# Query projection of cross attention: heads 1 to 3 by seven products of halves per pair of tiles

## The reference, cut to what matters

```python
def cross_attention(xn, mk, mv, w_xq, xq_norm, w_xo):
    bsz, t, _ = xn.shape
    q = rmsnorm((xn @ w_xq).reshape(bsz, t, N_HEADS_X, HEAD_DIM_X), xq_norm)
    s = jnp.einsum('bqhd,bkhd->bhqk', q, mk).astype(jnp.float32) * (HEAD_DIM_X ** -0.5)
    p = jax.nn.softmax(s, axis=-1).astype(mv.dtype)
    o = jnp.einsum('bhqk,bkhd->bqhd', p, mv).reshape(bsz, t, N_HEADS_X * HEAD_DIM_X)
    return o @ w_xo
```

## Time and profile before

| | |
|---|---|
| Median of three runs | 1535.73 us |
| Span of the profiled execution | 1531.5 us |
| Its own time | the span and what lies around it; the median is 4.2 us above the span |
| TensorE matmul busy | 1507.3 us, 98% |
| VectorE busy | 970.2 us, 63% |
| ScalarE busy | 592.3 us, 39% |
| GpSimd busy | 243.6 us, 16% |
| DMA | 189.33 MB, 124 GB/s |
| Granted TensorE clock | 9 tenths or more in all 40 slices |

### The profile page before, as it was taken

How to read it: one execution, slowest core, us unless ns; L and a number is a source line. 1 busy time by engine, 2 the same in 40 slices (tenths; PEclk the granted TensorE clock), 3 DMA queues, 4 the chain that set the end, 5 groups by cost and what they waited for, 6 DMA issues and landing times.

```text
span 1531.5 us, 26752 instructions
## 1 busy us (share of the span) xinstructions
PE 1507.3 (98%) x10928; PEld 1447.3 (95%) x10928; DVE 970.2 (63%) x1370; ACT 592.3 (39%) x1021; POOL 243.6 (16%) x322
## 2 busy tenths in 40 slices
PE   8999999999999999998999999999999999999998
PEld 8999999997778999986899999999999999999998
DVE  7736777757777443457443896666665597547653
ACT  7521031146775221235322743333334344334332
POOL 1010000002100100000000054455444310010110
PEclk9999999999999999999999999999999999999999
DMA  8425111103102533022212244443344865354562
GB/s 279 142 98 176 54 42 42 45 1 103 68 29 71 163 127 136 15 73 71 85 73 85 85 158 158 150 151 128 133 177 177 325 230 181 117 178 121 185 213 100
DMA packets 64063, 189.33 MB, mean 124 GB/s; under 512 B 7888, under 2 KB 12040, under 8 KB 63808
## 3 DMA queue, kind: packets, MB, share of 16 engines
q1 hardware_dynamic: 39392, 95.30, 19.0%
q0 software_dynamic: 24560, 92.45, 16.8%
HBM read 138.58 MB, written 54.12 MB: 126 GB/s over the span
## 4 chain that ended last, share of the span: by engine, by line
PE 50%; DMA 4%; DVE 2%; issue 1%; ACT 1%; SPq 0%; DVEq 0%
PE ps L2836 20%; PE ps L2857 19%; PE ps L424 8%; DMA a<-wdn 3%; PE ps L2709 1%; PE ps L2676 1%; DVE B_lo L1985 0%; DMA r_raw_a<-quads_d 0%; DVE neg_max L1946 0%; PE ps L2687 0%; PE ps L2716 0%; DVE xpt_lo L1992 0%; ACT x_scores L1288 0%; ACT B_hi L1329 0%; DVE w_lo_b L411 0%
## 5 line engine op out<-in xcount | busy, mean ns | idle before, releaser
L424 PE MATMUL ps<-A_hi,w_hi 128*128 128x364 f32 (+1 forms) x768 | 171.2, 331 | 0.3 <-DVE Y L1554 0.3
L424 PE MATMUL ps<-A_lo,w_hi 128*128 128x364 f32 (+1 forms) x768 | 169.0, 328 | 0.0
L424 PE MATMUL ps<-A_hi,w_lo 128*128 128x364 f32 (+1 forms) x768 | 168.3, 327 | 0.0
L387 ACT ACTIVATE w_hi<-w_raw 128x1024 fp32r<-128x1024 f32 x42 | 44.2, 1058 | 286.2 <-PE ps L424 185.7
L424 PEld LDWEIGHTS ps<-A_hi,w_hi 128*128 128x128 f32 x768 | 130.8, 188 | 7.3 <-issue 6.6
L424 PEld LDWEIGHTS ps<-A_lo,w_hi 128*128 128x128 f32 x768 | 132.8, 188 | 0.0
L424 PEld LDWEIGHTS ps<-A_hi,w_lo 128*128 128x128 f32 x768 | 132.6, 188 | 0.0
L391 DVE TENSOR_TENSOR w_lo<-w_raw,w_hi 128x1024 fp32r<-128x1024 f32 x42 | 51.1, 1221 | 101.9 <-ACT w_hi L387 101.9
L2836 PE MATMUL ps<-t_hi,wq_hi 128*128 128x272 f32 x480 | 99.3, 288 | 0.3 <-issue 0.3
L2836 PE MATMUL ps<-t_lo,wq_hi 128*128 128x272 f32 x480 | 99.2, 288 | 0.0
L2836 PE MATMUL ps<-t_hi,wq_lo 128*128 128x272 f32 x480 | 99.1, 288 | 0.0
(11 more groups left out here) (327 smaller groups left out, 3570.4 us busy)
## 6 DMA issues: line engine op xcount, KB each, us to landing
w_raw<-slabs SPq DMA_DIRECT2D x67, 512.0 KB, 4.0
quads_d<-quad_sum POOLq DMA_DIRECT2D x64, 272.0 KB, 2.9
w_raw<-wdn POOLq DMA_DIRECT2D x32, 512.0 KB, 4.1
r_raw_a<-quads_d SPq DMA_DIRECT2D x56, 272.0 KB, 3.1
r_raw_b<-quads_d SPq DMA_DIRECT2D x56, 272.0 KB, 3.2
quads_d<-hid_stage POOLq DMA_DIRECT2D x48, 272.0 KB, 2.8
Y<-xT POOLq DMA_DIRECT2D x16, 546.0 KB, 4.8
y_d<-Y POOLq DMA_DIRECT2D x16, 546.0 KB, 3.2
```

The lines of the kernel that those rows point to most:

```text
L387: e.activation(WH[:, par], RAW[:, par], ACT.Copy).then_inc(s.w_hi, 1)
L424: ins = e.matmul(PS[:, 3 * par + c, 0:n_], wt[:, wpar, w], xt[:, col:col + n_], start=(first and n == 0 and m == 0), stop=(last and n == l ...
```

## The change: what it does

Tiles 0 and 1 (head 0) stay plain tiles. Tiles 2 to 7 (heads 1 to 3) become three pairs of seven products each, 21 products, with the functions of the MLP's first product or copies of them. The sums of the activations are made with `norm_x` before the first pair, in the same memory that the MLP uses later. The weight sums and copies of products lie in parts of `A` that the products don't read (`XSW`, `XTMP`). All pairs share one weight buffer `RAW`: the first half of the next pair is loaded after four weight sums and four low parts of this pair, the second half after all seven low parts. The products run in plain order 0 to 6. The squares of heads 0 to 2 go into tiles 6 and 7 of `Y`. VectorE makes all the low parts, of the sums, of the weights and of the activations. The stat and the broadcasts of head h now stand between products, in banks 0 or 6 (`stat_bank`). The keys and values of memory (`load_kv`) of heads 0 to 2 are loaded when 17, 19 and 21 products are done, where they were loaded ahead of tile 2 before. Tile counts after the projection are six lower (`C_XO`, `C_UP`), and counts of the MLP's products start after those of the projection (`X_PROD` and the like).

```diff
+N_XPAIR = 3
+N_XPROD = 7 * N_XPAIR
 # SyncE
+            for p in range(N_XPAIR):
+                for half in range(2):
+                    if p == 0:
+                        sp.wait_ge(s.w_lo, S_XQ + half + 1)
+                    elif half == 0:
+                        sp.wait_ge(s.sp_sum, 4 * p)
+                        sp.wait_ge(s.sp_lo, 7 * p - 3)
+                    else:
+                        sp.wait_ge(s.sp_lo, 7 * p)
+                    sp.dma_start(RAW[:, half], slabs[S_XQ + 2 + 2 * p + half]).then_inc(w_in[half], 16)
             for h in range(3):
+                sp.wait_ge(s.prod, 17 + 2 * h)
                 load_kv(h)
...
 # ScalarE
+            quad_scaled(1, "norm_x", S_OUT + 8)
+            t_hi(0, 0)
             act_root(e, cnt, D)
+            quad_scaled(3, "norm_x", S_OUT + 8)
+            xleft_hi(0)
+            t_hi(1, 0)
             act_bcast(e, cnt, RSTD)
+            t_hi(2, 0)
+            xleft_hi(1)
+            xleft_hi(2)
+            xprod_copy(0)
+            xsquares(0)
+            xleft_hi(3)
+            xprod_copy(1)
+            t_hi(3, 0)
+            xleft_hi(4)
+            xprod_copy(2)
+            xleft_hi(5)
+            act_root(e, cnt, 256, bank=stat_bank(0))
+            cnt.bc += 2
+            xleft_hi(6)
+            for n in range(7, N_XPROD):
+                p, i = divmod(n, 7)
+                xprod_copy(n - 4)
+                xleft_hi(n)
+                if i == 3:
+                    xsquares(p)
+                if i == 5:
+                    act_root(e, cnt, 256, bank=stat_bank(p))
+                    cnt.bc += 2
...
-            for i in range(8):
-                if i < 6:
-                    act_split(e, S_XQ + i + 2, i % 2, S_XQ + i + 1)
...
 # VectorE
+            t_raw(0, "norm_x", 0, 0)
+            t_raw(1, "norm_x", 0, 0)
+            t_lo(0, 0)
             dve_recip(e, cnt)
             cnt.bc += 2
+            t_raw(3, "norm_x", 0, 0)
+            xleft_lo(0)
+            t_raw(2, "norm_x", 0, 0)
             e.wait_ge(s.bc_used, cnt.used(cnt.bc))
-            for i in range(8):
-                if i < 6:
-                    dve_split(e, S_XQ + i + 2, i % 2)
...
+            xevac(0)
+            xevac(1)
+            xleft_sum(1)
+            xleft_sum(2)
+            xleft_lo(1)
+            t_lo(1, 0)
+            xleft_lo(2)
+            xleft_sum(4)
+            xleft_lo(3)
+            xleft_lo(4)
+            t_lo(2, 0)
+            xleft_sum(5)
+            xleft_lo(5)
+            xcombine(3)
+            dve_recip(e, cnt)
+            t_lo(3, 0)
+            xleft_lo(6)
+            xcombine(4)
+            xq_nrm(0, 0)
+            xleft_lo(7)
+            xcombine(5)
+            xq_nrm(0, 1)
+            for n in (3, 4, 5):
+                xscale(n)
+            for n in (8, 9):
+                xleft_sum(n)
+                xleft_lo(n)
+            for n in range(10, N_XPROD):
+                p, i = divmod(n, 7)
+                xcombine(n - 4)
+                if n + 1 < N_XPROD:
+                    xleft_sum(n + 1)
+                xleft_lo(n)
+                xscale(n - 4)
+                if i == 5:
                     dve_recip(e, cnt)
+                if p == 2 and i < 2:
+                    xq_nrm(1, i)
...
 # TensorE, after tiles 0 and 1
-            for h in range(3):
-                xq_tile(2 * h + 2)
-                xq_stat(h)
...
+            for n in range(N_XPROD - 1):
+                p, i = divmod(n, 7)
+                xproduct(n)
+                if i == (2 if p == 0 else 1):
+                    if p == 1:
+                        e.wait_ge(s.u_rel, 4)
+                    xq_stat(p)
+                    n_rc += 1
+                if i == (4 if p == 0 else 3):
+                    pe_bcast(e, cnt, 0, rc_wait(n_rc), lo=stat_bank(p))
+                if i == (5 if p == 0 else 4):
+                    pe_bcast(e, cnt, 1, lo=stat_bank(p))
...
+            xscores(0)
+            xproduct(N_XPROD - 1, (0,))
+            xscores(1)
+            xproduct(N_XPROD - 1, (1,))
+            xscores(2)
+            xproduct(N_XPROD - 1, (2, 3))
```

More of the change, by code:

```diff
@@ L1273, in _, with quad_scaled @@
             for par in range(2):
-                residual(S_OUT, 0, par, "norm_x", 8)
+                residual(S_OUT, S_OUT, 0, par, "norm_x", 8)
             with e.Fori(1, 4) as i:
                 for par in range(2):
-                    residual(S_OUT, i, par, "norm_x", 8)
+                    residual(S_OUT, S_OUT, i, par, "norm_x", 8)
+            def quad_scaled(i, norm, count):
+                if i == 1:
+                    e.wait_ge(s.tile_done, count)
+                    e.wait_ge(s.tile_read, count)
+                lo = 0 if i == 1 else HT
+                for k in range(4):
+                    e.activation(TX[i][:, k], y(k)[:, lo:lo + HT], ACT.Copy, scale=par_col(norm, k)).then_inc(s.t_x, 1)
@@ L1446, in _ @@
             hidden_std(1)
-            t_hi(3)
+            t_hi(3, X_TF)
             left_hi(5)
@@ L1959, in xnorm, with t_raw @@
                     .then_inc(s.x_p, 1)
+            def t_raw(i, norm, x0, t0):
+                lo, hi = slice(0, HT), slice(HT, 2 * HT)
+                for k in range(4):
+                    g1, g2 = par_col(norm, k), par_col(norm, k + 4)
+                    if i == 0:
+                        e.wait_ge(s.t_x, x0 + k + 1)
+                        src, g, sub = y(k)[:, hi], g1, TX[1][:, k]
+                    elif i == 1:
+                        e.wait_ge(s.t_f, t0 + k + 1)
+                        src, g, sub = y(k + 4)[:, hi], g2, TF[0][:, k]
+                    elif i == 3:
+                        e.wait_ge(s.t_f, t0 + 4 * T_RAW.index(1) + k + 1)
+                        src, g, sub = y(k + 4)[:, lo], g2, TF[1][:, k]
+                    else:
+                        e.wait_ge(s.t_x, x0 + 4 + k + 1)
+                        src, g, sub = y(k + 4)[:, hi], g2, TX[3][:, k]
+                    e.scalar_tensor_tensor(TF[i][:, k], src, g, sub, ALU.mult, ALU.subtract).then_inc(s.t_f, 1)
@@ L1961, in _, with xscale @@
+            def xscale(n):
+                p, i = divmod(n, 7)
+                if i not in (3, 4, 5):
+                    return
+                half = QUAD[i][1]
+                e.wait_ge(s.u_add, 3 * p + i - 2)
+                e.tensor_tensor(xq_quad(n), xq_quad(n), RSTD[:, half * HT:(half + 1) * HT], ALU.mult).then_inc(s.u_rel, 1)
+            t_raw(0, "norm_x", 0, 0)
+            t_raw(1, "norm_x", 0, 0)
+            t_lo(0, 0)
             dve_recip(e, cnt)
             cnt.bc += 2
+            t_raw(3, "norm_x", 0, 0)
@@ L1979, in xo_lo @@
+            xcombine(17)
+            xq_nrm(2, 0)
+            xscale(17)
+            xcombine(18)
+            xq_nrm(2, 1)
+            xscale(18)
+            xcombine(19)
+            xmin(0)
+            xscale(19)
+            xmin(1)
+            xnorm(0)
+            xmin(2)
+            xcombine(20)
+            xnorm(1)
             def xo_lo(q):
@@ L2194, in _ @@
             left_lo(1)
-            t_lo(1)
+            t_lo(1, X_THI)
             left_lo(2)
```

419 lines of the change are left out of this document (247 added, 172 removed).

## The result

The changed kernel takes 1537.48 us in the median of 20 runs (1535.91 to 1542.73), the kernel before 1534.91 us (20 runs, 1532.32 to 1537.58) in the same session. The ratio is 1.0021, 95% interval 1.0014 to 1.0027: 3.2 us slower, with 2.1 to 4.1 us as the interval; the two medians by themselves differ by 2.6 us. The forecast was 3.2 us slower. The mechanism is as forecast, and so are the sizes of its terms. One term that I counted at nothing is there: falls of TensorE's clock.

What follows compares the result with a forecast made beforehand. TensorE, busy 1507.3 of 1531.5 us, was taken as the bound. Matmuls saved -8.2, new waits +11.1 and the end +0.3 gave +3.2 us, so 1538.9 us; the 8-in-10 range was 1531.5 to 1542.5.

Steps and rivals of the forecast that it cites:

- term 1: TensorE's matmuls in the query projection: 432 plain ones (71.5 us) replaced by 504 cheaper ones (63.3 us), -8.2 us.
- (a): Broadcast in tile 1: TensorE waits for VectorE's splits and reciprocal, 1.7 us.
- (c): First broadcast of head 0: TensorE waits for a chain over ScalarE and VectorE ending in the reciprocal, 2.0 us.
- (d): Second broadcast of head 0: TensorE waits for the half norm that reads the first broadcast, 1.9 us.
- (f): Stat of head 1: TensorE waits for a chain through product 6's scale and the squares, 1.9 us.
- (g): Second broadcast of head 1: the norm comes behind the load of pair 2's second half, TensorE waits 2.6 us.
- term 2: Seven new TensorE waits in the query projection for operands from other engines, taken to add: +11.1 us.
- term 3: End of the projection: the last squares wait for the last product's scale, +0.3 us, bounds 0 and 0.6.
- rival 3: TensorE's clock falls in wait (g) or another, adding 3 to 6 us: 1542 to 1545; chance 0.06.
- rival 4: Shared weight buffer: the load in (g) lands late, adding 2.2 to 4.7 us: 1541 to 1543.6; chance 0.07.
- rival 1: The other engines' added work is hidden, as at the MLP's start: 1528.5 us; chance 0.12.
- rival 2: The projection's waits exist but are half as long, 5.6 us: 1533.4 us; chance 0.17.

Runs made afterwards that it cites:

- e6: The changed kernel without the query norms of heads 0 to 2; ratio 0.9919 to the kernel before, -12.4 us.
- e5: The kernel before without the query norms of heads 0 to 2; ratio 0.9949 to the kernel before as it was, -7.8 us.
- e11: The changed kernel run once more, unchanged; 1538.09 us, ratio 1.0023 to the kernel before.
- e7: The changed kernel with six unused matmuls filling TensorE's 2.8 us gap ahead of head 1's values; ratio 1.0018 to the kernel before, +2.8 us.
- e9: The changed kernel with only TensorE's part of the order e4, VectorE and ScalarE as they were; ratio 1.0032 to the kernel before, 4.9 us slower.
- e2: The changed kernel with VectorE's weight sum for product 15 moved behind head 1's half norm; ratio 0.9994 to the kernel before, 0.9 us faster.
- e4: The changed kernel's same instructions reordered on VectorE, ScalarE and TensorE within the projection; 1529.74 us, ratio 0.9961 to the kernel before.
- e1: The changed kernel with tile 1's two broadcasts after slices 5 and 6, not 3 and 4; ratio 1.0009 to the kernel before, 1.4 us slower.
- e3: The changed kernel with the edits of e1 and e2 together; ratio 0.9994 to the kernel before, -0.9 us.

## Why the prediction was right, point by point

| step | forecast, us | bracket, us | loss by the starts of rows, us | from |
|---|---|---|---|---|
| term 1, matmuls | -8.2 | | -8.3 | e6 against e5, with e6's waits |
| (a) first broadcast, tile 1 | 1.7 | 1.51 | 1.77 | trace of the change |
| (b) products 1 and 2 | 0.7 | 0.42 | 0.85 | the same |
| (c) first broadcast, head 0 | 2.0 | 1.74 | 2.00 | the same |
| (d) second broadcast, head 0 | 1.9 | 1.63 | 1.89 | e11 (hidden by a fall of the clock in the first) |
| (e) product 8 | 0.3 | none | 0.31 | trace of the change |
| (f) stat of head 1 | 1.9 | 1.61 | 1.68 | the same |
| (g) second broadcast, head 1 | 2.6 | 2.48 | 2.75 | the same (e11: 2.35 in brackets) |
| term 2, sum | 11.1 | 9.4 | 11.25 | the above |
| a wait of the kernel before that is gone | 0 | | -0.4 | 665.33 to 666.12 |
| term 3, the end | 0.3 | | 0.4 | stat of head 3 at 691.84, before 688.99, less 2.41 |
| clock | 0 | | 0 to 1.7 a fall | e7, e9, e11 |

**The mechanism was right.** The stage is 2.5 us longer (98.01 against 95.55), and the end 0.4: 2.9 of the 3.2 us. e2 and e4 show that the waits are the cause: with most of them gone, and the instructions the same, the change is worth 5.7 to 6.0 us.

**The sizes were right too.** The walk missed no wait by more than 0.2 us. Whoever adds up the numbers in brackets finds 9.4 us of waits and concludes that the matmuls saved only 7.4; both are misread, since each wait costs TensorE about 0.26 us more than its bracket says. Only (f) costs no more than 0.07 us beyond it, as a stat has such steps at its edges anyway (605.05 to 605.39 without a wait). The same reading closes three runs to 0.02 us: e1 (0.58 against 0.60), e2 ((g) falls from 2.75 to 0.49, and the stage by 2.26) and e4 (7.10 against 7.11 us of the stage). Luck was in the timed number: 3.2 against 3.2 us is closer than an interval of 2.1 to 4.1 can tell, and the falls of the clock might have added more.

**"Its pieces ... add" was half right.** (a) to (g), term 1 and the wait that is gone add up to the stage within 0.1 us, and e3 adds to within 0.01 us. But e1 shows that taking away a wait of 1.77 us gives 0.6: a wait is TensorE's distance to an engine that stays as late as it was. e9 is the clearest case.

**"I count no loss" was wrong, rival 3's mechanism is real.** The forecast rested on a single gap of 2.80 us without a fall and on the 40 slices of the page. The page can't show such a fall: a slice is 38 us long, and the changed kernel's page, with its two falls, has 9 in all 40 as well. In the fourteen profiles at hand, gaps of over 2 us in projection and attention were followed by a fall in 13 of 19 cases, and that very gap of 2.8 us in 8 of 12. A fall cost some 1.7 us, and not the 3 to 6 us of rival 3. In time it is small for this change: the runs' mean clock went from 0.9979 (before, all three later sessions) to 0.9966 and 0.9965, so 2 us more of full clock lost in a run, part of it behind waits. What it adds to the 2.9 us is 0.3 to 0.6 us by the ratios and nothing by the medians, so its share of the time is not shown.

**Rival 4, late loads**, fell: the load in (g) took 3.35 us, where the walk had 3.3, and the memory keys and values of heads 0 and 1 landed in 2.7 to 4.5 us, with no wait of TensorE for them. Rival 1 fell with the six gaps, rival 2's 5.6 us with the 11.2 measured. Of the signs named, products 0.126 us apart, the longest new gap, the gap ahead of head 1's stat and VectorE's 8 tenths came. The profile puts that gap down to "issue", but ScalarE's squares (628.87, 2.12 us long) end 0.1 us ahead of the stat at 631.09. "Busy time about 8 us lower" did not come (3.1): the two falls, in which matmuls are busy for longer, make up some 3.4 us of the difference, and the rest stays open. One sign that I had named as wrong did come, a granted clock below full in the stretch (0.50 from 616 to 618 us).

## What to carry to other kernels

Where an engine takes no break, work saved on it leaves less time to all that feed it. Walk each operand's chain from the last common event, and order the feeding engines by who is wanted next. An instruction that waits for a load holds up all behind it on its engine: put it behind whatever is wanted sooner, as in e2, where one place was worth 2.3 us. Move the order of all engines together: TensorE's half alone won nothing in the stage, VectorE's and ScalarE's 3.0 us, and both together 7.1. And take what a wait costs from the starts of the rows around it, not from the idle time in brackets.

## What the runs showed of the hardware

In these traces the fall of the clock behind a gap is not tied to a place. All 15 falls in the projection and attention of the fourteen profiles stand behind a gap. Of 42 gaps of 1.5 to 1.8 us two were followed by one (e9 and the changed kernel's first profile, both behind 1.74 us), of 19 of 2.2 to 2.9 us thirteen. What decides in a given execution no run here shows. The same kernel had it behind 1.74 us in one execution and behind 2.35 us in another. Each took about 1.7 us of full clock, in e3 once twice as much. The Trainium skill, "TensorE: Matmul & The Clock Gate", section "Why this matters for your kernels", says that idle gaps between bursts of matmuls send the clock back to its lower level. The traces agree that each fall has a gap ahead of it; of the 61 gaps counted here, 15 were followed by one. A single trace without a fall says little about a gap, and that is where my forecast went wrong: it took one row for a proof.
